# Output weight blocks: low parts by ScalarE and an accumulating DMA in place of GpSimd, and first output products one turn later

## The reference

```python
for l in range(DEPTH):                      # DEPTH = 2
    proj = einsum('bld,de->ble', h, w_in[l])
    a, g, zc, q, k, v, za, qi, ki, wi = split(proj, IN_SPLITS)
    y_conv = conformer_conv_branch(a, g, zc, ...)          # depthwise conv, layer norm, silu, gate
    q, k, qi, ki = apply_rope(...)
    y_attn = dsa_sparse_attention(q, k, v, qi, ki, wi, topk) * silu(za)   # top 132 keys of each row
    y = einsum('ble,ed->bld', concatenate([y_conv, y_attn], -1), w_out[l])
    h = layer_norm(ALPHA * h + y, post_ln_g[l], post_ln_b[l])
# second block: rmsnorm, one product w_in, grouped-query attention, gated MLP, merge, w_out, rmsnorm
```

## Time and profile before

| | us |
|---|---|
| median of 3 runs | 1025.79 (1024.05 to 1026.18) |
| the profiled execution | 1024.52 |
| its span | 1022.6 |
| TensorE busy | 987.3 |
| VectorE busy | 667.8 |
| ScalarE busy | 558.8 |
| GpSimd busy | 231.4 |

### The profile page before, as it was taken

How to read it: one execution, slowest core, us unless ns; L and a number is a source line. 1 busy time by engine, 2 the same in 40 slices (tenths; PEclk the granted TensorE clock), 3 DMA queues, 4 the chain that set the end, 5 groups by cost and what they waited for, 6 DMA issues and landing times.

```text
span 1022.6 us, 15789 instructions
## 1 busy us (share of the span) xinstructions
PE 987.3 (97%) x6084; PEld 816.8 (80%) x6084; DVE 667.8 (65%) x1439; ACT 558.8 (55%) x915; POOL 231.4 (23%) x250
## 2 busy tenths in 40 slices
PE   7999999998999999999999999999999999999997
PEld 7888988886677988888778677888888788888886
DVE  3899999888674489999988756638422333333432
ACT  6685891645333558588165534544646566564442
POOL 0110771115211401077111512634101000000001
PEclk9999999999999999999999899999999999999999
DMA  8876874752001577488464400577777536365662
GB/s 301 196 180 179 210 181 131 166 124 83 1 1 50 157 177 176 124 185 187 124 171 79 156 21 1 171 180 188 176 210 197 114 89 158 90 158 126 175 155 82
DMA packets 23098, 143.92 MB, mean 141 GB/s; under 512 B 2785, under 2 KB 3297, under 8 KB 7281
## 3 DMA queue, kind: packets, MB, share of 16 engines
q0 software_dynamic: 8496, 60.36, 31.7%
q1 hardware_dynamic: 14528, 82.55, 22.8%
HBM read 140.81 MB, written 2.10 MB: 140 GB/s over the span
## 4 chain that ended last, share of the span: by engine, by line
PE 81%; ACT 7%; DVE 5%; DMA 3%; POOL 2%; issue 2%; SPq 0%; POOLq 0%; DVEq 0%; ACTq 0%
PE psum_B L1371 21%; PE psum_A L1371 14%; PE psum_B L1406 7%; PE psum_A L1406 7%; PE psum_A L1568 6%; PE psum_C L1448 3%; PE psum_A L1786 2%; PE psum_B L1568 2%; PE psum_B L1786 2%; PE psum_A L1484 2%; PE psum_B L1512 2%; DVE conv_acc L1887 2%; POOL w_lo L1155 2%; PE psum_B L1773 2%; PE psum_C L1371 1%
## 5 line engine op out<-in xcount | busy, mean ns | idle before, releaser
L1162 POOL DMA_DIRECT2D w_lo<-in_weights x59 | 52.0, 881 | 562.2 <-ACT w_lo L706 536.0
L1887 DVE SCALAR_TENSOR_TENSOR conv_acc<-u,vec,conv_acc 128x528 f32<-128x528 f32 (+1 forms) x240 | 172.3, 755 | 3.2
L1371 PE MATMUL psum_B<-x_hi,w_hi 128*128 128x264 f32 (+3 forms) x472 | 143.9, 338 | 2.5 <-DVE mlp_lo L2341 1.2
L1371 PE MATMUL psum_B<-x_lo,w_hi 128*128 128x264 f32 (+3 forms) x472 | 141.7, 333 | 0.0
L1371 PE MATMUL psum_B<-x_hi,w_lo 128*128 128x264 f32 (+3 forms) x472 | 141.2, 332 | 0.0
L705 ACT ACTIVATE w_hi<-w_raw 128x2048 fp32r<-128x2048 f32 (+2 forms) x73 | 113.4, 1553 | 18.7 <-DMA w_raw<-in_weights 18.2
L1371 PE MATMUL psum_A<-x_hi,w_hi 128*128 128x264 f32 (+3 forms) x408 | 111.1, 311 | 2.0 <-DVE za L2041 0.9
L706 ACT ACTIVATE w_lo<-w_raw 128x2048 fp32r<-128x2048 f32 (+2 forms) x73 | 112.7, 1544 | 0.0
L1371 PE MATMUL psum_A<-x_lo,w_hi 128*128 128x264 f32 (+3 forms) x408 | 109.1, 306 | 0.0
L1371 PE MATMUL psum_A<-x_hi,w_lo 128*128 128x264 f32 (+3 forms) x408 | 109.0, 305 | 0.0
L1371 PEld LDWEIGHTS psum_B<-x_hi,w_hi 128*128 128x128 f32 (+1 forms) x472 | 82.1, 186 | 13.4 <-issue 3.7
(11 more groups left out here) (407 smaller groups left out, 2199.5 us busy)
## 6 DMA issues: line engine op xcount, KB each, us to landing
w_raw<-in_weights SPq DMA_DIRECT2D x66, 1024.0 KB, 5.0
w_lo<-in_weights POOLq DMA_DIRECT2D x57, 1024.0 KB, 8.6
h<-in_x SPq DMA_DIRECT2D x1, 2048.0 KB, 11.0
out<-h SPq DMA_DIRECT2D x4, 512.0 KB, 2.6
x_first<-in_x_t SPq DMA_DIRECT2D x3, 528.0 KB, 8.3
post_ln_g<-in_post_ln_g SPq DMA_DIRECT2D x2, 512.0 KB, 4.7
post_ln_b<-in_post_ln_b SPq DMA_DIRECT2D x2, 512.0 KB, 6.1
w_raw<-in_weights SPq DMA_DIRECT2D x2, 288.0 KB, 6.4
```

What stands on the lines that cost most here:

```text
L1162: pool.dma_start(wlo[n % RING][:, 0:width], io["weights"][n, :, 0:width], accum_op=ALU.add) \
L1371: mm = pe.matmul(ps[0:cols, i, 0:b - a], w[wp][:, kt, at:at + cols], x[xp][:, kt, a:b], start=(kt == 0 and wp + xp == 0), stop=(kt == KD - ...
L1887: got = dve.scalar_tensor_tensor(dst, src, w, dst, ALU.mult, ALU.add)
```

## The change

Four weight blocks leave `LO_BY_POOL`: `("wo", 0, 1)` and `("wo", 1, 1)` of both layers. ScalarE writes high part and negated copy of each half, one half at each of the turns 13, 15, 17 and 19, and GpSimd issues the accumulating DMA at turn 15 for the one block and at turn 19 for the other. The first output products of layer 0 move from turns 17, 19 and 22 to 19, 21 and 23; the first of layer 1 from turn 17 to 18.

```diff
 OUTPUT_AT = {
-    0: ((17, 0, 0, "A"), (19, 0, 1, "B"), (22, 1, 0, "A"), (25, 1, 1, "B"), (27, 0, 2, "A"), (29, 1, 2, "A"),
+    0: ((19, 0, 0, "A"), (21, 0, 1, "B"), (23, 1, 0, "A"), (25, 1, 1, "B"), (27, 0, 2, "A"), (29, 1, 2, "A"),
         (34, 0, 3, "A"), (36, 1, 3, "A")),
-    1: ((17, 0, 1, "A"), (19, 0, 2, "B"), (21, 1, 1, "A"), (23, 1, 2, "A"), (26, 0, 3, "A"), (28, 1, 3, "A")),
+    1: ((18, 0, 1, "A"), (19, 0, 2, "B"), (21, 1, 1, "A"), (23, 1, 2, "A"), (26, 0, 3, "A"), (28, 1, 3, "A")),
 }
-LO_BY_POOL = {NUMBER[key] for key in ((0, "wo", 0, 1), (0, "wo", 1, 1), (1, "a", 0), (1, "g", 0),
-                                      (1, "wo", 0, 1), (1, "wo", 1, 1), (2, "kv", 0), (2, "q", 0))}
+LO_BY_POOL = {NUMBER[key] for key in ((1, "a", 0), (1, "g", 0), (2, "kv", 0), (2, "q", 0))}
 SPLITS_AT = {
-    0: ((0, 1, ("zc", 2)), (2, 3, ("wo", 0, 0)), (5, 6, ("wo", 1, 0)), (12, 13, ("wo", 0, 1)), (17, 19, ("wo", 1, 1))),
-    1: ((0, 1, ("zc", 2)), (2, 3, ("wo", 0, 0)), (7, 8, ("wo", 1, 0)), (12, 13, ("wo", 0, 1)), (17, 17, ("wo", 1, 1))),
+    0: ((0, 1, ("zc", 2)), (2, 3, ("wo", 0, 0)), (5, 6, ("wo", 1, 0)), (13, 15, ("wo", 0, 1)), (17, 19, ("wo", 1, 1))),
+    1: ((0, 1, ("zc", 2)), (2, 3, ("wo", 0, 0)), (7, 8, ("wo", 1, 0)), (13, 15, ("wo", 0, 1)), (17, 19, ("wo", 1, 1))),
 }
```

## The result

| | before | after |
|---|---|---|
| median, us | 1025.74 (1024.05 to 1026.18, 4 runs) | 1031.68 (1031.31 to 1032.14, 4 runs) |
| profiled execution, us | 1024.52 | 1031.85 |
| its span, us | 1022.6 | 1029.8 |

A forecast was written before the change was run, and what follows sets the result against it. TensorE, busy 97% of the span, was taken as the bound. Layer 0's 3.8, its clock's 0.5 and layer 1's -0.3 gave +4.0 us: 1028.5 against the profile, 1029.8 as median with 1.3 added; 8 in 10: 1026.4 to 1031.8 us.

The forecast's parts named there:

- the largest term: Layer 0, turns 17 to 19: the moved tile 0 product no longer covers the round, a loss of 3.8 us.
- the taking of turn 16: Layer 0: ScalarE takes turn 16's probabilities at 240.8 us against 240.42, VectorE's 1.5 us gain being spent on ScalarE.
- TensorE stands idle for nearly that time: Layer 0, before turn 19: without the moved product TensorE idles for nearly its 3.8 us length.
- the clock, taken as 0.5: Layer 0: low clock after two longer idle stretches adds 0.5 us, bounds -0.3 to 1.7.
- The rival in which the clock takes more: Low stretches follow both layer 0 holes: 1.2 us more, as much in layer 1, 1031 to 1032 us; chance 0.12.
- wait for nothing: Layer 1: the first product moves only past turn 18's transposition and `v` products, claimed unwaiting, so no hole opens.
- Layer 1 comes to -0.5 + 0.2 = -0.3 us: Layer 1's sum: 0.5 us gained at turn 17, 0.2 us stall for the low part's DMA; range -2.4 to +2.
- The gain at turn 17: Layer 1: ScalarE takes turn 16 at 575.9 against 576.40 us, gaining 0.5 us at turn 17.
- the late low part: Rival: layer 1's DMA, slowed by table loads, lands at 587 us or after, +2 us, 1031.5 us; chance 0.10.
- have no slack to win back: Layer 0's later products move back by the same 3.8 us, with their low parts there in time.
- The two signs named as refuting the prediction: Layer 0's turn 19 starting before 247 us, or layer 1's L1568 wait for the low part reaching 2 us.
- The second sign: Layer 1: a TensorE wait of 2 us or more on the `w_lo` DMA at L1568 would refute the prediction.

The follow-up runs named there:

- l0_only: The change in layer 0 alone (splits and output turns), layer 1 as in the kernel before: 1031.05 us, ratio 1.0054 to the kernel before.
- outputs_only: Kernel before with only the output turns moved as in the change, low parts still by GpSimd: 1029.64 us, ratio 1.0040.
- l1_best: Kernel before with layer 1 alone changed, its first block split at turns 12 and 13, first product at 18: 1026.23 us, ratio 1.0004.
- place18: Kernel before with layer 0's first output product moved from turn 17 to 18, splits by GpSimd: 1026.49 us, ratio 1.0009.
- l1_only: The change in layer 1 alone, layer 0 as in the kernel before: 1028.05 us, ratio 1.0022 to the kernel before.
- place17_23: Kernel before with layer 0's third output product moved from turn 22 to 23, first still at 17: 1026.30 us, ratio 1.0011.
- cover18: Changed kernel with the first block split at turns 12 and 13 in both layers, layer 0's products at 18, 19, 23: 1030.19 us, 1.0038 to before.
- early_dma: Kernel before with the four blocks split by ScalarE and DMA, first block at turns 12 and 13, output turns unmoved: 1027.99 us, ratio 1.0022.
- tables_late: Changed kernel with layer 1's post-norm vector and second-block table loads held until turn 18's product: 1032.09 us, ratio 1.0075 to the kernel before.
- l1_early: Changed kernel with layer 1's first block split at turns 12 and 13, its DMA two turns earlier: 1029.13 us, ratio 1.0045 to the kernel before.
- fill: Changed kernel with unused matmuls in layer 0's two waits, 12 at turn 16 and 15 at turn 18: 1032.66 us, ratio 1.0085 to the kernel before.

## Why the prediction was right and wrong

- **Direction and the largest term: right.** Layer 0's stretch is 3.98 us longer in the profiled pair, 4.3 was forecast (3.8 + 0.5); by the ratio of l0_only, over more executions, it costs 5.5 us (4.0 to 7.1). outputs_only shows that the places of the products hold most of it: they alone cost 4.1 us. VectorE's shorter step, ScalarE's second passes, and the taking of turn 16 (241.23 us, forecast 240.8) and of turn 18 (248.66, forecast 248.3) came as worked out, with 0.55 us in each for the later start of the stretch; turn 19 started at 249.14 us, forecast "about the same" as 249.07.
- **Its split: wrong.** "TensorE stands idle for nearly that time" (3.8 us) measured +2.24 us, and turn 19's own wait 1.55 us where 3 to 4 stood; the clock, taken as 0.5, +1.74. The holes were filled in part by the same matmuls running slow. The rival in which the clock takes more was in substance what layer 0 did, without changing its sum by much. l0_only's low clock of 13.7 us and the spread of l1_best show that this part is not the same in each execution.
- **One cause was overlooked.** The prediction says that in layer 1 "turn 18's transposition and products with `v`" are what "wait for nothing". The products wait for VectorE to read bank B: 0.6 us in layer 0 of after and 0.7 in layer 1. A product at turn 17 stands ahead of them and covers this wait. place18, in which the product is one turn later and the splits are unchanged, shows it open (1.1 us), and turn 17's transposition back for L1997 as well (0.7 us).
- **The step that failed: "Layer 1 comes to -0.5 + 0.2 = -0.3 us".** The gain at turn 17 was there: from the gate product to turn 17's transposition 8.87 us after and 9.48 before, -0.6. But from that transposition to turn 19's product 15.95 us after against 12.99 before, +2.96, where +0.2 stood. Of that 1.05 us are the wait for the DMA, which took 11.8 us instead of the 8.7 to 9.7 of the earlier trace rows, 0.7 us that for `y_part`, and 0.6 us one of turn 17's transposition back for L1996, which was hidden before. The rest, 0.6 us, is net of a low clock that now lies over the product's first half (4.27 us, where half of the earlier trace rows's is 3.2). I had put the crowding of the landing at nothing in the value and at +2 in the bound. The rival "the late low part" ("lands at 587 us or after: +2 us", 0.10) is thus what came in layer 1: the low part landed at 592.8 us, which is 588.1 us on before's time scale, as the stretch starts 4.7 us later. l1_only and l1_best fit it: 2.3 us (1.2 to 3.4) with the DMA at turn 15, 0.4 (-0.5 to 1.3) with it at turn 13. They don't part the landing from the moved passes.
- **The other products of layer 0, "have no slack to win back": incomplete.** Moving the third from 22 to 23 costs 1.1 us by itself (place17_23, 0 to 2.3) and opens two waits, 1.0 and 0.8 us. In after no wait shows there, as turn 21's product stands ahead; what of this price after pays is open.
- **The base.** I put the new median 1.3 us above its own profile, as before's was. It lies 0.2 below. The profiled pair differs by 7.3 us, the medians by 5.9, so against the profile from which it was worked out the forecast is 3.3 us short. The allowance of 1.3 us, which didn't hold, brought the median's miss down to 1.9: luck. Of before's 28 executions measured beside cover18, the time that would be lost to the clock if TensorE had worked all through, (1 - mean granted clock) x time, is 6.1 us on average; of after's four it is 10.8. So up to some 4.8 us of the 5.9 lie in the low clock (an upper estimate, as it also counts low clock over idle time), which a forecast from one profile can't fix to the microsecond.

The two signs named as refuting the prediction (turn 19 before 247 us, a wait of 2 us or more at L1567) did not come; the time still missed the forecast by 1.9 us, at the edge of the range. The second sign could not tell: the low clock over the product's first half hid most of the DMA's delay, and the same delay stood as 3.1 us in l1_only. What stays open: why the clock's low stretches in layer 0 last 3.4 us in some executions and 6.8, 10.2 or 13.7 in others of kernels with nearly the same waits, and why the moves of the two products cost 3.1 us together and 2.0 as a sum (the intervals allow both).

## What to carry to other kernels

In this kernel, filler work on a busy TensorE had a place, and its worth was every wait that came right behind it: before moving a product one turn, list the waits of all instructions that it now stands behind, also those that show no wait today because the product covers them. Moving work from an engine that disturbs another to one that is nearly late can win nothing, even if the sum of its busy time is small: in layer 0 two passes more of 0.95 us, on an engine that is 55% busy in all, took back what VectorE won at turn 15 (ScalarE took turn 16 at 240.7 us on before's time scale, against 240.42). Price a DMA by its landing beside the same traffic, not by that of the same DMA in a quiet stretch.

## What the runs showed of the hardware

- The accumulating DMA of 1 MB took 8.0 us from issue to landing where the core's DMAs moved 131 to 134 GB/s in that time (early_dma's second, tables_late's first of layer 1), and 11.0 to 12.4 us where they moved 240 to 250 GB/s and where loads of vectors and tables ran beside it (tables_late's second 11.0, early_dma's 11.8 and 12.4, l1_early's 12.1). Between these the rate doesn't order them: 8.5 us at 210 GB/s (after at 203 us), 9.7 at 192 (before at 202 us), 11.8 at 200 (after at 581 us, beside such loads).
- A VectorE `tensor_scalar` with one tensor input (128x272) took 0.62 us where it began beside a GpSimd subtraction of 128x1024, 1.05 us beside a GpSimd `TENSOR_TENSOR` of 128x512, 0.36 us without.
- A low clock of 3.4 to 13.7 us lay in layer 0's stretch in each profile, with 3.0 to 6.2 us of idle time in the stretch (fill apart), and the longest didn't go with the most idle time. In one execution, twelve filler matmuls in a wait of 3 us moved its start from 242.0 to 246.5 us; over four executions the mean granted clock was as without them, but for that one.
